# Norms and gating of the heads, output projection, second norm and router of a hybrid diffusion layer in one stage of slots over token tiles

## What is computed

```python
# RWKV heads: 6 heads of 64; o[0], o[1] are the two scan directions
o = o[0] + o[1]
on = (o - mean(o)) * rsqrt(var(o) + 64e-5) * ln_w + ln_b
o_rw = (on + bonus) * gate
# GLA heads: 4 heads of 96 (in column-major grid order)
o = o[0] + o[1]
o_gla = o * rsqrt(mean(o * o) + 1e-6) * norm_w * silu(g)
# layer
out = concat([o_lru, o_rw, o_gla], -1) @ w_out      # 256 + 384 + 384 channels
x = x + g1 * out
h = rmsnorm(x, norm2_g) * (1 + sc2) + sh2
probs = softmax(h @ w_router)                         # 16 experts
```

## Time and profile before

| | us |
|---|---|
| median of three runs | 3913.74 (3909.47 to 3916.18) |
| the profiled execution | 3920.33 |
| its span, first to last instruction | 3918.7 |
| mean granted TensorE clock | 0.908 of full |

### The profile page before, as it was taken

How to read it: one execution, slowest core, us unless ns; L and a number is a source line. 1 busy time by engine, 2 the same in 40 slices (tenths; PEclk the granted TensorE clock), 3 DMA queues, 4 the chain that set the end, 5 groups by cost and what they waited for, 6 DMA issues and landing times. The chain is left out here.

```text
span 3918.7 us, 92410 instructions
## 1 busy us (share of the span) xinstructions
PE 3257.4 (83%) x37497; PEld 2927.1 (75%) x37497; DVE 2347.6 (60%) x4616; ACT 1613.2 (41%) x2838; POOL 827.5 (21%) x1188
## 2 busy tenths in 40 slices
PE   5879989999679999999613995199999999999990
PEld 2857766666569999999512774199999999999990
DVE  3554548984457777777685556555555555555542
ACT  2313655564434444444342332144444444444432
POOL 0100000000236666666210000111111111121001
PEclk8989989998789999999855997599999999999995
DMA  5444336554524444444265442355556655566536
GB/s 177 128 146 162 78 92 202 181 185 131 162 59 101 100 100 98 101 100 100 75 195 186 137 139 91 116 174 184 183 173 184 195 183 183 173 199 184 180 119 199
DMA packets 599065, 573.57 MB, mean 146 GB/s; under 512 B 212561, under 2 KB 541585, under 8 KB 597789
## 3 DMA queue, kind: packets, MB, share of 16 engines
q1 hardware_dynamic: 569136, 471.87, 40.9%
q0 software_dynamic: 29616, 97.26, 8.1%
HBM read 425.05 MB, written 143.95 MB: 145 GB/s over the span
## 5 line engine op out<-in xcount | busy, mean ns | idle before, releaser
L3053 DVE TENSOR_TENSOR exp_wlo<-exp_raw,exp_whi 128x2048 fp32r<-128x2048 f32 x192 | 440.4, 2294 | 374.1 <-ACT exp_whi L3006 374.1
L3006 ACT CAST exp_whi<-exp_raw 128x2048 fp32r<-128x2048 f32 x192 | 365.6, 1904 | 95.5 <-DMA exp_raw<-in_w_gate 95.5
L954 PE MATMUL mix_acc<-proj_hThi,mix_wlo 128*128 128x448 f32 (+3 forms) x920 | 365.9, 398 | 14.3 <-DVE mix_wlo L1279 14.3
L954 PE MATMUL mix_acc<-proj_hTlo,mix_whi 128*128 128x448 f32 (+3 forms) x920 | 341.8, 372 | 0.0
L954 PE MATMUL mix_acc<-proj_hThi,mix_whi 128*128 128x448 f32 (+3 forms) x920 | 340.9, 371 | 0.0
L2941 PE MATMUL exp_g<-exp_xThi,exp_wlo 128*128 128x272 f32 x1024 | 298.6, 292 | 10.1 <-DVE exp_xTlo L3057 8.9
L2941 PE MATMUL exp_o<-exp_hidhi,exp_wlo 128*128 128x272 f32 x1024 | 305.2, 298 | 0.0
L2941 PE MATMUL exp_g<-exp_xThi,exp_whi 128*128 128x272 f32 x1024 | 296.8, 290 | 0.0
L2941 PE MATMUL exp_o<-exp_hidhi,exp_whi 128*128 128x272 f32 x1024 | 296.7, 290 | 0.0
L2941 PE MATMUL exp_u<-exp_xThi,exp_wlo 128*128 128x272 f32 x1024 | 296.5, 290 | 0.0
L2941 PE MATMUL exp_u<-exp_xThi,exp_whi 128*128 128x272 f32 x1024 | 296.2, 289 | 0.0
(11 more groups left out here) (368 smaller groups left out, 8663.4 us busy)
## 6 DMA issues: line engine op xcount, KB each, us to landing
exp_raw<-in_w_gate SPq DMA_DIRECT2D x64, 1024.0 KB, 5.4
exp_raw<-in_w_up SPq DMA_DIRECT2D x64, 1024.0 KB, 5.3
exp_raw<-in_w_down SPq DMA_DIRECT2D x64, 1024.0 KB, 5.3
scn_plain<-rec SPq DMA_DIRECT2D x68, 384.0 KB, 3.6
rec<-mix_arena SPq DMA_DIRECT2D x24, 896.0 KB, 4.2
proj<-mix_out POOLq DMA_DIRECT2D x88, 224.0 KB, 2.6
scn_grc<-grec SPq DMA_DIRECT2D x136, 128.0 KB, 3.9
mix_arena<-in_w_ada SPq DMA_DIRECT2D x12, 1024.0 KB, 5.8
```

The costliest lines, as they stand in the source:

```text
L954: mm = pe.matmul(acc[n % ACCS][0:width, 0:tn], wt[:, k, 0:width], hT[hp][:, k, t0:t0 + tn], start=k == 0 and i == 0, stop=k == KD - 1 and ...
L3006: act.copy(w[k % RING][0][:, :, :], raw[k % RAW][:, :, :]).then_inc(hi_done[k % RING], 1)
L3053: dve.tensor_tensor(w[k % RING][1][:, :, :], raw[k % RAW][:, :, :], w[k % RING][0][:, :, :], ALU.subtract).then_inc(lo_done[k % RING], 1)
```

## The change

`stage_post` and the call of it go. `stage_mix_out` takes its inputs and does both. The order is now by slots: in slot s an engine runs, in a fixed order, steps of tile s - b, where b is the step's distance; there are 17 + 7 slots, and all of it is written out, with no hardware loop. The heads' results go into `m_raw` in SBUF instead of through `mixT`; only the 256 LRU rows are loaded from there. The channel weights of RWKV are applied by ACT (Identity with scale and bias) instead of DVE. The squares go into the buffers `rw_ob`, `gl_ob`. The product has one pair of PSUM banks instead of two. The loads of `w_out` and its split lie in slots 0 and 1, the scale rows in slot 2. The instructions are the same otherwise.

```diff
+        ps_o, ps_t = [st.ps(f"o{half}") for half in range(2)], [st.ps(f"t{half}") for half in range(2)]
+        ps_l, ps_p, ps_rw, ps_gl = st.ps("l"), st.ps("p"), st.ps("rw_t"), st.ps("gl_t")
...
+        def each_slot(*steps):
+            for s in range(TILES + LAST):
+                for behind, step in steps:
+                    t = in_slot(s, behind)
+                    if t is not None:
+                        step(t, t % 2)
...
+                load_rw(0, 0)
+                load_gl(0, 0)
+                sp.dma_start(ident[:, :], ident_d).then_inc(par_in, 16)
+                for j in range(UN):
...
+                load_w(0)
+                load_w(1)
+                load_rw(1, 1)
+                load_gl(1, 1)
+                for t in range(2):
+                    load_gates(t, t)
+                    load_lru(t, t)
+                load_w(2)
+                load_w(3)
                 load_modulated_norm(sp, rows_in, (g_row, scale_row, shift_row), mods, norm2_g, 4, 3)
...
+                each_slot((3, after(load_x)), (0, after(load_rw)), (1, after(load_gates)), (0, after(load_gl)), (1, after(load_lru)))
...
+                each_slot((3, store_y), (3, store_h))
...
+                def product(t, u):
+                    if t == 0:
+                        pe.wait_ge(w_low, PARTS)
+                    pe.wait_ge(m_low, t + 1)
                     for half in range(2):
                         cols = slice(half * BANK, (half + 1) * BANK)
+                        if t:
+                            pe.wait_ge(left, 2 * (t - 1) + half + 1)
...
+                each_slot((2, product), (4, route), (3, turn), (0, turn_heads), (6, turn_probs))
...
+                def affine(t, u):
...
+                    for j in range(UN):
+                        act.activation(m_raw[u][:, LRU_K + j, :], ps_rw[:, j * P:(j + 1) * P], ACT.Identity, bias=rw_par[:, 1, j:j + 1],
+                                       scale=rw_par[:, 0, j:j + 1]).then_inc(rw_affine, 1)
+
+                def high(t, u):
+                    act.wait_ge(lru_in[u], 16 * (t // 2 + 1))
+                    act.wait_ge(rw_mixed, t + 1)
+                    act.wait_ge(gl_mixed, t + 1)
...
+                def exponential(t, u):
+                    act.wait_ge(ntop, t + 1)
...
+                each_slot((1, affine), (4, copy_h), (3, square), (0, rw_square), (5, exponential), (3, take_root), (0, gl_square), (0, roots), (1, high),
+                          (0, silu), (0, split_weights))
...
+                def residual(t, u):
...
+                    for half in range(2):
                         cols = slice(half * BANK, (half + 1) * BANK)
+                        dve.wait_ge(mixed, 2 * t + half + 1)
+                        dve.tensor_tensor(y1[u][:, cols], ps_o[half][:, :], res_row[:, min(t, 1), cols], ALU.mult).then_inc(left, 1)
...
+                def gated(t, u):
+                    dve.wait_ge(rw_affine, UN * (t + 1))
+                    dve.wait_ge(gates_in[u], 32 * (t // 2 + 1))
...
+                dve.wait_ge(par_in, N_PAR)
+                each_slot((4, copy_h), (3, residual), (5, top_logit), (0, rw_centre), (3, mean_square), (0, gl_add), (5, softmax), (3, norm), (0, variances),
+                          (1, gated), (0, heads_normed), (1, low), (0, split_weights), (7, keep_probs))
...
-    stage_post(nc, o_rw, bonus, gate, a["rw_ln_w"], a["rw_ln_b"], o_gla, proj, a["gla_norm_w"], a["ident"], mixT)
```

More of the change, by code:

```diff
@@ L2289, in stage_post @@
[L2289 to L2307, removed]
@@ L2445, in stage_mix_out @@
-def stage_mix_out(nc, x_prompt, x_sample, mixT, w_out, mods, norm2_g, w_router, ident_d, y, h2, probs_lat, probs_ctx):
-    PW = 2 * P
-    PARTS = D // PW
-    with Stage(nc, "out") as st:
-        ident = st.sb("ident", [P, P])
+        rw_of, rw_ob, rw_cen, gl_of, gl_ob = ([st.sb(f"{x}{u}", [P, D_RW]) for u in range(2)] for x in ("rw_of", "rw_ob", "rw_cen", "gl_of", "gl_ob"))
+        rw_bo, rw_ga, gl_ga = ([st.sb(f"{x}{u}", [P, UN, P]) for u in range(2)] for x in ("rw_bo", "rw_ga", "gl_ga"))
@@ L2532, in product, with turn @@
-                        mm.then_inc(mixed[u], 1)
-                def route(u, n, tile, seg):
-                    pe.wait_ge(h_ready[u], n)
-                    for half in range(2):
-                        pe.wait_ge(copied[half], tile)
+                                mm = pe.matmul(ps_o[half][:, :], m[u][mp][:, k, :], wo[wp][:, k, cols], start=k == 0 and i == 0, stop=k == KD - 1 and i == 2)
+                        mm.then_inc(mixed, 1)
+                def turn(t, u):
+                    pe.wait_ge(h_ready, t + 1)
+                    for half, copied in enumerate((copied0, copied1)):
+                        if t:
+                            pe.wait_ge(copied, t)
@@ L2559, in _ @@
                     act.copy(wo[0][:, :, q * PW:(q + 1) * PW], w_raw[q % 2][:, :, :]).then_inc(w_high, 1)
-                def split(u, n, tile, seg):
-                    act.wait_ge(mix_in[u], 16 * n)
-                    act.wait_ge(mixed[u], 2 * (n - 1))
-                    act.copy(m[u][0][:, :, :], m_raw[u][:, :, :]).then_inc(m_high[u], 1)
-                def norm(u, n, tile, seg):
-                    act.wait_ge(res_done[u], n)
-                    act.wait_ge(h_out[u], 16 * (n - 1))
-                    act.wait_ge(turned[1], tile - seg)
-                    act.activation(h[u][:, :], y1[u][:, :], ACT.Square, accum_out=ss[u][:, 0:1]).then_inc(sumsq[u], 1)
-                    act.wait_ge(meansq[u], n)
-                    act.activation(ss[u][:, 2:3], ss[u][:, 1:2], ACT.Sqrt).then_inc(root[u], 1)
@@ L2574, in softmax, with split_weights @@
-                def softmax(u, n, tile, seg):
-                    act.wait_ge(turned[1], tile + 1)
-                    act.copy(hT[u][:, 4:8, :], ps_t[1][:, :].rearrange("p (k t) -> p k t", k=4)).then_inc(copied[1], 1)
-                    act.wait_ge(ntop[u], n)
-                    act.activation(pe_exp[u][:, :], ps_l[:, 0:N_EXP], ACT.Exp, bias=ss[u][:, 5:6], accum_out=ss[u][:, 6:7]).then_inc(expd[u], 1)
-                staged(act, split, other_engines, norm, softmax)
+                def split_weights(t, u):
+                    if t < 2:
+                        split_w(2 * t)
+                        split_w(2 * t + 1)
@@ L2627, in keep_probs @@
[L2627 to L2630 removed]
+                        dve.wait_ge(mixed, 2 * t + half + 1)
+                        dve.tensor_tensor(y1[u][:, cols], ps_o[half][:, :], res_row[:, min(t, 1), cols], ALU.mult).then_inc(left, 1)
+                    dve.wait_ge(left, 2 * (t + 1))
```

460 lines of the change are left out of this document (239 added, 221 removed).

## The result

The changed kernel takes 3788.1 us (median of 4 runs, 3784.6 to 3789.7) against 3915.0 for the kernel before on the same chip: ratio 0.9676, 95% interval 0.9659 to 0.9692. The forecast was 3788 and the range 3764 to 3832. The profiled execution took 3784.6.

A forecast was written before the change was run, and what follows sets the result against it. Two consecutive stages, first DVE-bound, then PE-bound, took 480.4 us; fused, DVE sets an 18.1 us slot: 67.2 + 235.3 + 33.6 + 19.0 = 355.1, 125.3 less, giving 3795 profiled and 3788 us median, range 3764 to 3832.

The forecast's parts named there:

- The slot's sum: Fused stage, one slot: DVE's work of 15.2 us plus waits of 1.6 and 1.1, with 0.2 more, makes 18.1 us.
- The waits: DVE's list in each slot: 1.6 us before softmax for ACT's Exp, 1.1 us before norm for ACT's root.
- DVE's own list: DVE per slot without waits: 14.9 us busy plus 0.3 of gaps, 15.2, with bounds 14.4 and 16.0.
- The loop: PE per slot: residual 1.4, product 10.9, router 1.9, turning 1.0 make 15.2 us, or 16.8 with one clock dip.
- a dip in every slot: PE: about 7 us between products drops the clock to 1.2 GHz each slot, costing 1.6 us, hidden under DVE's 18.1.
- rival A: PE's clock returns late in each slot, making its loop 20.6 us; cost 40 us, kernel 3828; chance 17%.
- The start: Slots 0 to 3, with parameters, weight parts, scale rows and first product, take 67.2 us.
- Rival D: Start: heads' loads queue on SP's list behind weights, parameters, gates and rows; 87 us instead of 67, kernel 3808; chance 7%.
- The end: After slot 18: the earlier 22.6 us less 3.6 for the router of tile 15, giving 19 us.
- B: ACT's table switches each cost a drain, 2.8 us more per slot over 13 slots, 36 us, kernel 3824; chance 5%.
- C: DVE's two waits on ACT shrink, so PE's loop of 16.8 us bounds the slot; 17 us less, kernel 3771; chance 12%.
- E: PE's clock never returns between light stretches, 27.5 us a slot; 153 us more, kernel 3941, slower than before; chance 3%.

The follow-up runs named there:

- no waits: Changed kernel with Exp and root first on ACT, gating between softmax and norm and low part before heads' scaling on DVE: 3756.2 us, ratio 0.9586.
- router twice: Changed kernel with PE doing the router's eight products twice, the second overwriting the same values: 3804.5 us, ratio 0.9716.
- heads early: Changed kernel with the loads of the heads of tile 2 issued ahead of the seven rows and x: 3782.8 us, ratio 0.9660.
- three banks: Changed kernel with the product in three PSUM banks instead of two, router and probabilities sharing one: 3782.9 us, ratio 0.9661.
- Exp first: Changed kernel with ACT taking Exp and the norm's root ahead of the heads' square: 3763.0 us, ratio 0.9604.
- weights first: Changed kernel with all four weight parts loaded and split ahead of slot 0: 3784.9 us, ratio 0.9677.
- three banks and no waits: Changed kernel with ACT's and DVE's lists reordered to hide the Exp and root waits, plus three PSUM banks for the product: 3743.1 us, ratio 0.9552.

## Why the prediction was right

**What bounded it before.** Right: two stages with opposite bounds, one behind the other. The fusion is the gain: 131 us of the stage. With affine back on DVE the kernel is still 2.9% under the one before, and the move of affine alone gives nothing.

**The slot's sum.** Right in kind, 4% high in size: 18.1 was forecast, 17.38 measured. The waits were placed and sized well (1.6 and 1.1; measured 1.74 and 1.15). The term that was off is DVE's own list: 15.2, measured 17.38 - 1.74 - 1.15 = 14.5. Its part for gaps was right, 0.3 against 17.38 - 2.89 - 14.14 = 0.35. Too long was the busy time, 14.9 against 14.14: I added the busy times of the two stages, but in the mixed order more neighbours are independent and overlap. The recorded lengths of one slot add up to 15.4 and overlap by 1.25; those of one tile in both stages before, without affine, add up to 15.7 and overlap by about 0.7. The slots 4 to 16 took 223.6 where 235.3 was forecast: 9.4 us of the difference are the 0.72 a slot, and most of the rest is slot 4, which has no softmax yet and took 15.25. ACT (busy 10.0 a slot, under 11 forecast) and the loads (share 0.57, at most 0.63 forecast) stayed hidden; what `mixT` saves is 0.8 MB a slot and not 0.9.

**PE's slack.** The loop was forecast at 15.2, or 16.8 with a clock dip; where it sets the pace it takes 14.78 ("no waits"; slot 18 of the changed kernel) and 16.4 to 16.6 with a dip. So it was 0.4 high, and the slack was there, as the router twice confirms. But "a dip in every slot" failed: of the seven slots from 2062.6 to 2184.3 two had a clock of 0.90 and five 1.00, though PE was on short work or idle for 4.8 to 6.4 us in each. The trace of the kernel before spoke against the sign that I read there. I took the dip to come "in some tiles"; it came in every second one, though the 3.6 us without product stood in all of them. Two tiles one behind the other, from copy to copy:

```profile
2244.91:2259.46 14.55, 13.83 (x75) 11.68 (x74) 8.08 (x15) 5.81 (x9) 0.53 (x1) 1.00 0.41 123
2259.46:2275.62 16.16, 15.44 (x75) 12.80 (x74) 8.07 (x14) 5.92 (x9) 1.60 (x3) 0.89 0.43 148
```

So the second stage's tile took 14.55 and 16.16 in turn, and router, turning and waits between products are no sufficient sign of a dip. In the changed kernel it cost nothing up to slot 16, as PE had slack. The pattern that the Trainium skill describes ("TensorE: Matmul & The Clock Gate", HAM oscillation), named beside rival A, agrees with the late slots of the router twice, where each slot has a low stretch and a clock of 0.87, and not with the changed kernel.

**The start and the end.** 67.2 was forecast for the start, 72.5 measured. What I missed is the 6.29 us for the heads of tile 2: I counted only DVE, ACT and the weights, and not where on SP's list the next loads stood. The prediction's sentence that each load is issued over a slot ahead holds for the slots and fails in the start. Without that wait, in the kernel with the heads early, the start was 68.8. Rival D named this place and over-priced it (20 us). Slots 17 and 18: 31.4 against 33.6, as only slot 17 had a dip. The end: 21.9 against 19. I had taken off the router of tile 15, but it still stood ahead of the last turning; and the turning then waited 0.70 us more for DVE's norm, whose root stands behind Exp and its table load on ACT (without that load the slot took 9.25 instead of 11.57).

**The sum.** 349.4 against 355.1: +5.3 in the start, -11.7 in the slots, -2.2 and +2.9 behind them. The median came to 3788.1, on the forecast, while the profiled execution was 10 us below the 3795 that went with it; that the median matches to 0.1 us is luck. The stage was 5.7 us shorter than forecast and the unchanged code ahead of it 4.3; against that, I took 6.6 us off the profiled execution for the median, and the median lies 3.5 above it.

**The rivals.** A: not seen in the changed kernel, where a product's low stretch lasted up to 3.9 us, against the 5.3 of A, which no row gave. A long stretch came in the kernel with affine on DVE, 3.1 to 6.1 us of a product in every second slot, and was hidden there by DVE's 18.46; the router twice has the dip in each late slot but a loop of 18.3 and not 20.6. B: falls, by the table load taken out. C: falls, the waits are as long as walked. D: in part, 5 us. E: did not happen, the clock was 0.96 in the slots.

What stays open: which property of PE's work decides whether a slot has a dip. The slot's length alone does not: there was none at 15.88, but at 17.38 the dips came in two of seven slots of the changed kernel, in most slots with three banks and in none of the first six slots of the router twice. The light stretch between products alone does not either: 3.6 us stood ahead of a dip in every second tile of the kernel before, 4.9 us ahead of none with Exp first. No run isolates it.

## What to carry to other kernels

Where two stages with different busy engines stand one behind the other, put their tiles in one list of slots, and price the slot by the busiest engine's list plus each place where that list asks for something that another engine starts only in the same slot. Those places are then cheap to move: here the order of two lists, with no instruction added or removed, gave another 33 us of the stage on top of the change's 131, and only after that did a third PSUM bank pay in the slots. Read the start by the load queue's own list: one load behind seven large ones cost 3.7 us (10.7 with the weights first), while moving the four weight parts alone changed the start by 1.3.

## What the runs showed of the hardware that I had not expected

- An Identity activation of 128x128 from PSUM with scale and bias operands is recorded with 0.447 us, but three in a row take 1.14 to 1.16, since they overlap; I had put 0.37 each, 1.1 in all.
- An issue on SP took 7.29 us behind seven loads of 0.5 MB (4.2 to 7.2 in the other fused kernels), where those of the heads around it take 0.3 to 1.4.
- Sharing a PSUM bank between router and probabilities, with waits that keep the engines apart, cost no slot time where DVE sets the slot (17.38 with and without).
- Where DVE instructions of two independent tiles stand in one list, their records overlap: by 1.25 us in a slot of 32 instructions, against about 0.7 for the same work in two stages.
- PE was busy 140.0 of 140 us and DVE 135.9 with clock 1.00 in the kernel with three banks and no waits: both engines can be held full at once, with DMA at share 0.72.
